# The chunk recurrence of the gated linear attention (B heads): sums of all chunks first, states after them, output parts within chunks meanwhile

## The chip, the cores and the metric

The program runs on one core of a Trainium2 chip. The metric is the device time of one execution in microseconds, from the first to the last instruction of the core; smaller is better. TensorE (PE in the profile) multiplies and turns tiles, VectorE (DVE) and ScalarE (ACT) work on vectors, SyncE (SP) issues the loads of the weights. A core has one SBUF of 128 partitions and a PSUM of 8 banks of 512 float32 per partition, called `ps` here.

## What is computed

The reference is two transformer blocks on 512 tokens of width 1024: two layers with three kinds of heads and a SwiGLU, then two layers with a mixer and a mixture of experts each. The change is in one of the three kinds of heads of the first two layers, the gated linear attention `hgrn2_chunked` (4 heads of 64 by 64). It is shown here as the reference has it, for chunks of 64 tokens; the kernel takes chunks of 128.

```python
def step(state, inp):
    qt, lf, vt = inp
    kt = -jnp.expm1(lf)
    cum = jnp.cumsum(lf, axis=2)
    ...
    attn = jnp.einsum('bhtd,bhsd,bhtsd->bhts', qt, kt, decay)
    o = attn @ vt + jnp.einsum('bhtd,bhde->bhte', qt * jnp.exp(cum), state)
    last = cum[:, :, -1:, :]
    state = jnp.exp(last[:, :, 0, :, None]) * state + jnp.einsum('bhsd,bhse->bhde', kt * jnp.exp(last - cum), vt)
    return state, o
```

The output of a chunk has a part within the chunk (`attn @ vt`) and a part from the state before it. What a chunk adds to the state does not depend on the state. The state before the first chunk is zero.

## The kernel before

Each of the first two layers is a row of stages: `project_in`, `windows` (sliding attention), `hgrn` (the B heads), `delta` (the C heads), `project_out`, `swiglu`. Between stages PE, DVE and ACT meet at a barrier. Each engine has its own copy of each stage as a list of instructions written by hand, and they are tied by counting semaphores: `due("name")` gives the count to wait for, `signal` and `to("name", ...)` raise it, and `link` makes an engine wait for its own instruction. Each engine runs its list in order. The weights come as 1 MB panels through a ring of 8 places; SP issues a panel as soon as PE has released the place (`panel_used`), line 629.

The stage `hgrn` works on tiles with features on the partitions: two blocks `b` of 128 partitions, each with two heads `s` of 64 partitions, and 512 tokens in four chunks `c` of 128. Its first part builds the scores `attn` level by level, with four panels of modulation weights (`mod_panels`) multiplied in between. Its end, which the change touches, runs so:

- DVE line 2411 puts each token's distance to the end of its chunk into `b_d` (signal `b_qd`).
- ACT line 1770 takes `b_e` = exp(`b_cum`), line 1771 takes `b_d` = exp(-`b_d`) and signals `b_decay`, line 1772 takes each chunk's whole decay, lines 1775 and 1776 move score blocks between partitions (`b_spread`), `row_out(3, 7)` (line 1751) copies a modulation vector, and line 1779 copies the turned k out of PSUM banks 4 and 5 (`b_kdT_sb`).
- DVE waits for `b_decay`, then line 2413 multiplies `b_e` by q, line 2414 multiplies `b_d` by k (signal `b_kd`), line 2415 clears the state.
- PE turns `b_d` (`chunk_turns`, eight turns through line 655, signal `b_kdT`), turns the modulation vector (`mod_turn(3, 7)`, two turns), and then for each chunk, having waited for `b_state`: 16 products 64 columns wide into banks 0 and 1 (for each block, head and half of the chunk one of the state with the decayed q, and one of v with the scores, added in place), and, except in the last chunk, two products 128 columns wide of what the chunk adds (bank 4, signal `b_ds`). All go through `mm`, line 641. A float32 product is two records in the trace: 64-column products have the form `128*64 128x64`, the ones of what a chunk adds `128*128 128x128`.
- DVE, for each of the first three chunks, waits for `b_ds`, masks the sum by heads (line 2418), and takes the new state block by block (line 2421, two instructions), signal `b_state`. In the first chunk it also copies the modulation columns (`columns_out`, line 2334) after that.
- After the last chunk PE multiplies the identity by itself once (signal `b_out`), and ACT copies banks 0 and 1 to `mix` (line 1781). After the barrier `delta` begins with twelve small turns.

The loop of PE before, in short:

```python
for c in range(NT):
    pe.wait_ge(*due("b_state"))
    for b in range(2):
        for s in range(2):
            r = slice(s * 64, s * 64 + 64)
            for at, scores in ((c * P, b_left), (c * P + 64, b_near)):
                mm(ps[r, b, at:at + 64], b_s[:, b, r], b_e[:, b, at:at + 64], True, False)
                mm(ps[r, b, at:at + 64], b_vt[:, c, b * P + s * 64:b * P + s * 64 + 64],
                   scores[:, s, b * 4 + c, :], False, True)
```

`r` picks the half of the partitions of PSUM that a product writes, and so the half of the columns of the array that it uses: head `s` = 0 the lower, `s` = 1 the upper.

Of the kernel before, what the change touches and what calls it, by code (L numbers as in the profile page):

```python
# [11 lines left out]
ALU = mybir.AluOpType  # L12
# [6 lines left out]
P = 128  # L19
# [283 lines left out]
def build(nc, args, out, par):  # L303
    a = args
    general, first_t, even_t, pool_t = (packed(t)[1] for t in constants())
    with ExitStack() as ctx:
# [30 lines left out]
        def cut(buffer, start, size, **shape):  # L337

            v = buffer[:, start:start + size]
            if not shape:  # L340
                return v
            names_ = " ".join(shape)
            return v.rearrange(f"p ({names_}) -> p {names_}", **shape)
# [53 lines left out]
        b_vt, b_kdt = cut(work, 3072, 1024, c=4, f=256), cut(work, 4096, 1024, c=4, f=256)  # L397
        b_s, b_tmp = cut(work, 5120, 256, b=2, e=P), cut(work, 5376, 256, b=2, e=P)

# [235 lines left out]
        def _(pe):  # L635
# [276 lines left out]
            def hgrn(l):  # L912
# [31 lines left out]
                pe.wait_ge(*due("b_kdT_sb"))  # L944
                pe.wait_ge(*due("b_acc", 0))
                for c in range(NT):
                    pe.wait_ge(*due("b_state"))
                    for b in range(2):
                        for s in range(2):
                            r = slice(s * 64, s * 64 + 64)  # L950
                            for at, scores in ((c * P, b_left), (c * P + 64, b_near)):
                                mm(ps[r, b, at:at + 64], b_s[:, b, r], b_e[:, b, at:at + 64], True, False)
                                mm(ps[r, b, at:at + 64], b_vt[:, c, b * P + s * 64:b * P + s * 64 + 64],
                                   scores[:, s, b * 4 + c, :], False, True)
                    if c < NT - 1:
                        for b in range(2):
                            mm(ps[:, 4, b * P:b * P + P], b_kdt[:, c, b * P:b * P + P], b_vt[:, c, b * P:b * P + P],
                               True, True, "b_ds" if b else None)
                mm(ps[:, 5, 0:P], ident, ident, True, True, "b_out")

# [593 lines left out]
        def _(act):  # L1554
# [203 lines left out]
            def hgrn():  # L1758
                act.wait_ge(*due("b_v"))
                to("b_v_sb", f(b_vt, ps[:, 4:6, :].rearrange("p b (c f) -> p (b c) f", c=2), ACT.Copy))  # L1760
                for n in range(len(LEVELS)):
# [5 lines left out]
                    if n in (2, 5):  # L1767
                        row_out(1 + n // 3, 7)
                act.wait_ge(*due("b_qd"))
                link(f(b_e, b_cum, ACT.Exp))  # L1770
                to("b_decay", f(b_d, b_d, ACT.Exp, scale=-1.0))
                link(f(stats[:, 32:40].rearrange("p (b c) -> p b c", b=2),
                       b_cum.rearrange("p b (c t) -> p b c t", c=4)[:, :, :, P - 1], ACT.Exp))
# [415 lines left out]
        def _(dve):  # L2189
# [175 lines left out]
            def hgrn(l):  # L2365
# [45 lines left out]
                to("b_qd", tt(blocks_of(b_d, P), c, c[:, :, P - 1:P].to_broadcast([P, 8, P]), ALU.subtract))  # L2411
                dve.wait_ge(*due("b_decay"))
                link(tt(b_e, q, b_e, ALU.mult))
                to("b_kd", tt(b_d, z, b_d, ALU.mult))
                to("b_state", dve.memset(b_s, 0.0))
                for c in range(NT - 1):
                    dve.wait_ge(*due("b_ds"))
                    link(tt(b_tmp, ps[:, 4, 0:256].rearrange("p (b e) -> p b e", b=2),
                            halves.unsqueeze(1).to_broadcast([P, 2, P]), ALU.mult))
                    for b in range(2):  # L2420
                        i = stt(out=b_s[:, b, :], in0=b_s[:, b, :], scalar=stats[:, 32 + 4 * b + c:33 + 4 * b + c],
                                in1=b_tmp[:, b, :], op0=ALU.mult, op1=ALU.add)
                    to("b_state", i)
                    if c == 0:
                        columns_out(PLANS[f"layer{l}"], 3, 7)
                    due("b_state")
                due("b_state")
# [730 lines left out]
```

## Time and profile before

| what | value |
|---|---|
| runs | 3260.21, 3258.86, 3250.52 us |
| median | 3258.86 us |
| profiled execution | 3258.9 us, its span; nothing is shown around it |
| PE busy | 2947.2 us (90%) |
| DVE busy | 1062.4 us (33%) |
| ACT busy | 913.0 us (28%) |
| DMA | mean 196 GB/s, about 409 GB/s in the expert layers |
| granted TensorE clock | 0.962 of full speed in the mean |

How to read it: the busy shares say which engine works most, the chain of waits says which instruction ended last at each step, and the timeline gives start, duration, engine, line and, in square brackets, the idle time before an instruction and who ended it. The granted clock is given as a share of 2.4 GHz: 1.00 is 2.4 GHz and 0.50 is 1.2 GHz; a value between is a stretch with both.

### The profile page before, as it was taken

The numbers are of one execution on the slowest core, as the hardware profiler recorded it, in microseconds if no ns is written. First come the engines' busy times: TensorE is split into PE (matmuls) and PEld (weight loads), VectorE is DVE, ScalarE is ACT, GpSimd is POOL, SyncE is SP. The second block draws the span as 40 slices with busy tenths as digits, with TensorE's granted clock in tenths as the row PEclk, the third lists the DMA queues.
The fourth block names the chain that finished last, engine by engine and source line by source line (L and its number), as shares of the span: only waits on it lengthen the run. The fifth ranks groups of instructions, "written<-read, shape, count | busy, mean of one in ns | idle before, by whom it ended". The sixth has DMA issues, their size and how long they took to land.

```text
span 3258.9 us, 41546 instructions
## 1 busy us (share of the span) xinstructions
PE 2947.2 (90%) x18407; PEld 2024.4 (62%) x18407; DVE 1062.4 (33%) x1573; ACT 913.0 (28%) x1498; POOL 0.2 (0%) x4
## 2 busy tenths in 40 slices
PE   6997899999998799999989998889898887999897
PEld 3765768888776677888767766654443454444443
DVE  3445642233545653224243244420010135000002
ACT  3443242232444333223243354221110032110011
POOL 0000000000000000000000000000000000000000
PEclk9998999999999899999989999989999998999999
DMA  7224323323223422322263105479999953999997
GB/s 273 78 104 156 105 65 95 99 88 97 78 90 113 156 71 78 101 93 91 94 217 124 39 1 207 142 291 410 409 407 408 406 210 117 388 409 409 403 408 291
DMA packets 251539, 637.28 MB, mean 196 GB/s; under 512 B 12896, under 2 KB 110176, under 8 KB 251232
## 3 DMA queue, kind: packets, MB, share of 16 engines
q1 hardware_dynamic: 248224, 627.22, 51.9%
q10 hardware_dynamic: 3136, 7.40, 0.6%
q8 instruction: 146, 2.39, 0.3%
q14 instruction: 33, 0.27, 0.0%
HBM read 632.48 MB, written 2.10 MB: 195 GB/s over the span
## 4 chain that ended last, share of the span: by engine, by line
PE 70%; DMA 12%; DVE 7%; ACT 5%; PEld 2%; issue 2%; PEldq 1%; SPq 1%; ACTq 0%; DVEq 0%
PE ps L641 67%; DMA ring<-in_w_exp_up 6%; DMA ring<-in_w_exp_gate 5%; PE ps L655 3%; PEld ps L641 2%; ACT h L1653 1%; ACT mix_halves L1656 1%; PEldq L1112 1%; DMA ring<-in_ada_w 1%; SPq L629 0%; DVE work L2394 0%; DVE work L3038 0%; DMA ring<-in_w_mod 0%; DVE small L2952 0%; DVE work L2954 0%
## 5 line engine op out<-in xcount | busy, mean ns | idle before, releaser
L641 PE MATMUL ps<-mix_halves,work_halves 128*128 128x512 f32 (+1 forms) x1544 | 622.5, 403 | 44.7 <-DVE h_halves L2245 34.4
L641 PE MATMUL ps<-h_halves,work_halves 128*128 128x512 f32 (+1 forms) x1544 | 609.7, 395 | 6.2 <-DVE mix_halves L2245 3.9
L641 PE MATMUL ps<-mix_halves,ring_halves 128*128 128x512 f32 x1448 | 569.1, 393 | 0.0
L641 PE MATMUL ps<-ring,work 128*64 128x512 f32 x1552 | 395.5, 595 | 57.5 <-DMA ring<-in_w_exp_up 31.6
L2245 DVE TENSOR_TENSOR ring_halves<-ring,work_halves 128x2048 fp32r<-128x2048 f32 (+2 forms) x125 | 252.6, 2021 | 551.9 <-ACT work_halves L1576 453.5
L641 PEld LDWEIGHTS ps<-mix_halves,work_halves 128*128 128x128 f32 (+1 forms) x1544 | 291.1, 189 | 131.9 <-issue 49.2
L641 PEld LDWEIGHTS ps<-h_halves,work_halves 128*128 128x128 f32 (+1 forms) x1544 | 291.9, 189 | 73.8 <-issue 6.4
L641 PEld LDWEIGHTS ps<-mix_halves,ring_halves 128*128 128x128 f32 x1448 | 273.0, 189 | 60.8
L641 PEld LDWEIGHTS ps<-ring,work 128*64 128x64 f32 x1552 | 129.5, 137 | 270.7 <-issue 269.2
L1576 ACT ACTIVATE work_halves<-ring 128x2048 fp32r<-128x2048 f32 x102 | 188.2, 1845 | 336.7 <-PE ps L641 336.1
L641 PE MATMUL ps<-ring,proj 128*64 128x512 f32 (+1 forms) x1136 | 231.2, 546 | 3.1 <-issue 3.0
L2645 DVE SCALAR_TENSOR_TENSOR x<-ps,small,x 128x512 f32<-128x512 f32 x112 | 81.1, 748 | 291.5 <-PE ps L641 291.3
L641 PEld LDWEIGHTS ps<-ring,proj 128*64 128x64 f32 (+1 forms) x1136 | 81.4, 131 | 131.9 <-issue 126.2
L641 PE MATMUL ps<-proj_halves,work_halves 128*128 128x512 f32 x352 | 136.9, 389 | 0.0
L3010 DVE TENSOR_TENSOR work<-proj,ps 128x1024 f32<-128x1024 f32 x16 | 19.5, 1221 | 345.6 <-PE ps L641 345.6
L2080 ACT ACTIVATE work<-ps,small 128x128 f32<-128x128 f32 x128 | 48.2, 457 | 288.0 <-PE ps L641 288.0
L641 PE MATMUL ps<-proj,work 64*64 64x64 f32 (+3 forms) x1008 | 116.6, 325 | 13.3 <-issue 6.5
L641 PE MATMUL ps<-work,proj 64*64 64x64 f32 (+3 forms) x1488 | 113.1, 254 | 15.2 <-ACT proj L2050 3.4
L641 PEld LDWEIGHTS ps<-work,mix 128*128 128x128 f32 x1024 | 119.1, 197 | 11.0 <-issue 8.1
L641 PE MATMUL ps<-h_halves,ring_halves 128*128 128x512 f32 x320 | 125.8, 393 | 0.0
L641 PE MATMUL ps<-work,mix 128*128 128x128 f32 x1024 | 121.7, 281 | 2.6 <-DVE work L2978 2.6
L641 PE MATMUL ps<-ring,mix 128*32 128x256 f32 x1280 | 87.7, 421 | 33.8 <-DVE mix L2217 20.4
(396 smaller groups left out, 3405.7 us busy)
## 6 DMA issues: line engine op xcount, KB each, us to landing
ring<-in_w_exp_down SPq DMA_DIRECT2D x110, 1024.0 KB, 16.3
ring<-in_w_exp_gate SPq DMA_DIRECT2D x106, 1024.0 KB, 11.0
ring<-in_w_exp_up SPq DMA_DIRECT2D x88, 1024.0 KB, 15.2
ring<-in_ada_w SPq DMA_DIRECT2D x48, 1024.0 KB, 7.4
ring<-in_w_mod SPq DMA_DIRECT2D x48, 1024.0 KB, 7.5
ring<-in_w_in SPq DMA_DIRECT2D x22, 1024.0 KB, 5.3
ring<-in_w_gate SPq DMA_DIRECT2D x22, 1024.0 KB, 5.3
ring<-in_w_up SPq DMA_DIRECT2D x22, 1024.0 KB, 5.3
```

Of the source, the lines that this page charges most:

```text
L641: i = pe.matmul(o, lhsT, rhs, start=start, stop=stop, **kw)
L655: t = pe.transpose(o, i, ident[0:n, 0:n])
L1112: pe.drain().then_inc(sem["stage"], 1)
L1576: to("hi", f(rounded(panel_high(splits[0])), slot(n), ACT.Copy))
L1653: to("h", f(h_[:, k, :], h_[:, k, :], ACT.Identity, scale=scale[:, k:k + 1], bias=shift[:, k:k + 1]))
L1656: to("hi", f(rounded(hi[:, k, :]), h_[:, k, :], ACT.Copy))
L2080: i = f(x_sel[:, k, :], ps[:, 6 + half, k % 4 * P:k % 4 * P + P], ACT.Identity, scale=coef[:, 1, k:k + 1], bias=mod[:, l, 3, k:k + 1])
L2245: to("lo", tt(rounded(v), v, rounded(hi), ALU.subtract))
L2645: to(done, stt(out=x[:, m, :], in0=ps[:, bank, :], scalar=gate[:, m:m + 1], in1=x[:, m, :], op0=ALU.mult, op1=ALU.add))
L3010: to("e_act", tt(e_act, e_tmp, ps[:, 2:4, :].rearrange("p b f -> p (b f)"), ALU.mult))
```

## The change

For each layer's `hgrn` stage:

- ACT takes exp(-`b_d`) first, with its own signal, then exp(`b_cum`), also with a signal. DVE multiplies `b_d` by k after the first, signals `b_kd`, and multiplies `b_e` by q after the second.
- PE issues what all three chunks add in one run (six products of 128 columns, banks 4 and 5, one signal at the end), then the output parts within all four chunks (32 products of 64 columns, the two heads in turn), and then, for chunks 1 to 3, waits for the state and issues four products of 128 columns each. The products with the zero state of chunk 0 and the product of the identity are gone; the last product gives `b_out`.
- DVE copies the modulation columns before it waits for `b_ds`; then it masks the first sum right into the state after chunk 0 (signal), masks the other two into `b_tmp`, and takes the two further states with two instructions each. The clearing of the state is gone. Three states and three sums have places of their own.

```diff
--- before.py
+++ after.py
@@ -395,7 +395,7 @@
         b_near, b_far = (cut(work, at, 1024, s=2, g=8, t=64) for at in (1024, 2048))
         b_mask, b_left = cut(proj_all, 0, 7 * 64, n=7, t=64), cut(proj_all, 1024, 1024, s=2, g=8, t=64)
         b_vt, b_kdt = cut(work, 3072, 1024, c=4, f=256), cut(work, 4096, 1024, c=4, f=256)
-        b_s, b_tmp = cut(work, 5120, 256, b=2, e=P), cut(work, 5376, 256, b=2, e=P)
+        b_s, b_tmp = (cut(work, at, 768, c=3, b=2, e=P) for at in (5120, 5888))
 
         g_Ac, g_Ar, g_Tc, g_Yc = (cut(work, 1024 * i, 1024, g=16, t=64) for i in range(4))
         g_Xc, g_Y = cut(proj_all, 2048, 1024, g=16, t=64), four(work, 4096)
@@ -943,20 +943,24 @@
                 pe.wait_ge(*due("b_spread"))
                 pe.wait_ge(*due("b_kdT_sb"))
                 pe.wait_ge(*due("b_acc", 0))
+                for c in range(NT - 1):
+                    for b in range(2):
+                        at = c % 2 * 256 + b * P
+                        mm(ps[:, 4 + c // 2, at:at + P], b_kdt[:, c, b * P:b * P + P], b_vt[:, c, b * P:b * P + P],
+                           True, True, "b_ds" if c == NT - 2 and b else None)
                 for c in range(NT):
+                    for b in range(2):
+                        for at, scores in ((c * P, b_left), (c * P + 64, b_near)):
+                            for s in range(2):
+                                mm(ps[s * 64:s * 64 + 64, b, at:at + 64], b_vt[:, c, b * P + s * 64:b * P + s * 64 + 64],
+                                   scores[:, s, b * 4 + c, :], at == 0, False)
+                for c in range(1, NT):
                     pe.wait_ge(*due("b_state"))
                     for b in range(2):
                         for s in range(2):
                             r = slice(s * 64, s * 64 + 64)
-                            for at, scores in ((c * P, b_left), (c * P + 64, b_near)):
-                                mm(ps[r, b, at:at + 64], b_s[:, b, r], b_e[:, b, at:at + 64], True, False)
-                                mm(ps[r, b, at:at + 64], b_vt[:, c, b * P + s * 64:b * P + s * 64 + 64],
-                                   scores[:, s, b * 4 + c, :], False, True)
-                    if c < NT - 1:
-                        for b in range(2):
-                            mm(ps[:, 4, b * P:b * P + P], b_kdt[:, c, b * P:b * P + P], b_vt[:, c, b * P:b * P + P],
-                               True, True, "b_ds" if b else None)
-                mm(ps[:, 5, 0:P], ident, ident, True, True, "b_out")
+                            mm(ps[r, b, c * P:c * P + P], b_s[:, c - 1, b, r], b_e[:, b, c * P:c * P + P], False, c == NT - 1,
+                               "b_out" if c == NT - 1 and b and s else None)
 
             def delta(l):
 
@@ -1767,8 +1771,8 @@
                     if n in (2, 5):
                         row_out(1 + n // 3, 7)
                 act.wait_ge(*due("b_qd"))
-                link(f(b_e, b_cum, ACT.Exp))
                 to("b_decay", f(b_d, b_d, ACT.Exp, scale=-1.0))
+                to("b_decay", f(b_e, b_cum, ACT.Exp))
                 link(f(stats[:, 32:40].rearrange("p (b c) -> p b c", b=2),
                        b_cum.rearrange("p b (c t) -> p b c t", c=4)[:, :, :, P - 1], ACT.Exp))
                 near, far, left = (v.rearrange("p s g t -> p (s g t)") for v in (b_near, b_far, b_left))
@@ -2410,20 +2414,23 @@
                 c = blocks_of(b_cum, P)
                 to("b_qd", tt(blocks_of(b_d, P), c, c[:, :, P - 1:P].to_broadcast([P, 8, P]), ALU.subtract))
                 dve.wait_ge(*due("b_decay"))
+                to("b_kd", tt(b_d, z, b_d, ALU.mult))
+                dve.wait_ge(*due("b_decay"))
                 link(tt(b_e, q, b_e, ALU.mult))
-                to("b_kd", tt(b_d, z, b_d, ALU.mult))
-                to("b_state", dve.memset(b_s, 0.0))
-                for c in range(NT - 1):
-                    dve.wait_ge(*due("b_ds"))
-                    link(tt(b_tmp, ps[:, 4, 0:256].rearrange("p (b e) -> p b e", b=2),
-                            halves.unsqueeze(1).to_broadcast([P, 2, P]), ALU.mult))
+                columns_out(PLANS[f"layer{l}"], 3, 7)
+                dve.wait_ge(*due("b_ds"))
+                added = ps[:, 4:6, :].rearrange("p k f -> p (k f)")[:, 0:768].rearrange("p (c b e) -> p c b e", c=3, b=2)
+                mask = halves.unsqueeze(1).to_broadcast([P, 2, P])
+                to("b_state", tt(b_s[:, 0, :, :], added[:, 0, :, :], mask, ALU.mult))
+                for c in (1, 2):
+                    i = tt(b_tmp[:, c, :, :], added[:, c, :, :], mask, ALU.mult)
+                link(i)
+                for c in (1, 2):
+                    dve.wait_ge(*due("b_state"))
                     for b in range(2):
-                        i = stt(out=b_s[:, b, :], in0=b_s[:, b, :], scalar=stats[:, 32 + 4 * b + c:33 + 4 * b + c],
-                                in1=b_tmp[:, b, :], op0=ALU.mult, op1=ALU.add)
+                        i = stt(out=b_s[:, c, b, :], in0=b_s[:, c - 1, b, :], scalar=stats[:, 32 + 4 * b + c:33 + 4 * b + c],
+                                in1=b_tmp[:, c, b, :], op0=ALU.mult, op1=ALU.add)
                     to("b_state", i)
-                    if c == 0:
-                        columns_out(PLANS[f"layer{l}"], 3, 7)
-                    due("b_state")
                 due("b_state")
 
             def project_in(l):
```

## Rows read from the trace of the kernel before

**Rows 1.** The page, part 4, chain that ended last: shares of the span by engine.

```profile
PE 70%; DMA 12%; DVE 7%; ACT 5%; PEld 2%; issue 2%; PEldq 1%; SPq 1%; ACTq 0%; DVEq 0%
```

**Rows 2.** The chain of waits, layer 0, stage hgrn's end: start us, us, what.

```profile
285.33 1.06 ACT h L1770
...
287.51 1.24 DVE h L2413
...
288.77 1.24 DVE h L2414
...
290.14 2.37 PE ps L655 x10
...
293.24 3.71 PE ps L641 x36
...
309.61 1.02 ACT mix L1781
```

**Rows 3.** The chain of waits, layer 1, first and last of that end.

```profile
1084.82 3.71 PE ps L641 x36
...
1101.33 1.02 ACT mix L1781
```

**Rows 4.** Timeline, layer 0: what ACT and PE do around the turns.

```profile
289.67 0.36 ACT L1751 ACTIVATE mix<-ps 128x256 f32<-128x256 f32 x1
...
290.14 1.94 PE L655 MATMUL ps<-consts,h 128*128 128x128 f32 x8 [4.46 <-DVE h L2414]
...
291.88 0.63 PE L655 MATMUL ps<-consts,mix 128*128 128x128 f32 x2
292.12 1.02 ACT L1779 ACTIVATE work<-ps 128x1024 f32<-128x1024 f32 x1 [2.09 <-PE ps L655]
```

**Rows 5.** Windows, layer 0: us, busy PE, PEld, DVE, ACT, POOL; PEclk, DMA share, GB/s.

```profile
285.00:290.00 5.00, 0.59 (x2) 0.11 (x1) 2.75 (x3) 4.57 (x6) 0.00 (x0) 0.89 1.03 409
...
293.00:305.00 12.00, 9.42 (x101) 8.63 (x102) 2.15 (x7) 0.14 (x1) 0.00 (x0) 0.50 0.28 89
...
306.00:307.00 1.00, 0.45 (x4) 0.25 (x3) 0.48 (x2) 0.00 (x0) 0.00 (x0) 1.00 0.00 0
...
312.00:317.00 5.00, 4.66 (x17) 3.19 (x16) 3.49 (x12) 4.35 (x13) 0.00 (x0) 0.58 0.00 0
```

**Rows 6.** Timeline of PE: 64-column products, the two heads overlapping, 1.2 and 2.4 GHz.

```profile
294.18 0.48 PE L641 MATMUL ps<-h,work 128*64 128x64 f32 x4
...
294.67 0.48 PE L641 MATMUL ps<-h,work 128*64 128x64 f32 x4
...
308.18 0.34 PE L641 MATMUL ps<-h,work 128*64 128x64 f32 x4
...
308.47 0.33 PE L641 MATMUL ps<-h,work 128*64 128x64 f32 x4
```

**Rows 7.** Timeline of PE, stage delta, layer 0: 128-column products of two heads.

```profile
384.66 0.69 PE L641 MATMUL ps<-proj,work 128*64 128x128 f32 x4
385.08 0.69 PE L641 MATMUL ps<-h,work 128*64 128x128 f32 x4
385.71 1.22 PE L641 MATMUL ps<-work,proj 128*128 128x128 f32 x4
...
404.44 0.40 PE L641 MATMUL ps<-h,work 128*64 128x128 f32 x4
404.65 0.44 PE L641 MATMUL ps<-proj,work 128*64 128x128 f32 x4
```

**Rows 8.** Groups of instructions by form, 293 to 310 us: xcount, busy us, mean ns.

```profile
L641 PE MATMUL ps<-h,work 128*64 128x64 f32 x64 | 8.4, 304 | 4.2 <-DVE work L2421 3.5 <-issue 0.7
...
L2421 DVE SCALAR_TENSOR_TENSOR work<-work,small 128x128 f32<-128x128 f32 x6 | 1.8, 349 | 0.1
L2418 DVE TENSOR_TENSOR work<-ps,consts 128x256 f32<-128x256 f32 x3 | 1.3, 425 | 14.0 <-PE ps L641 14.0
```

**Rows 9.** Who waited for whom, SP's own queue, whole span.

```profile
SPq L629 <- PE ps L641: 2766.8, 388, 116.7
```

## The prediction

> **What bounds the kernel now.** I read the chain that ended last first: seven tenths of the span are PE, and DVE and ACT have a few per cent each [rows 1]. So a change to one short stage can only matter if that stage itself stands on the chain. The chain of waits over the stage shows that it does, without a gap: two exponentials on ACT, two products on DVE, the turns on PE, four rounds of PE and DVE, and the copy to `mix` [rows 2]. From the first product (293.24) to that copy (309.61) it takes 16.37 us in layer 0, and in layer 1 16.51 us (1084.82 to 1101.33) [rows 3]. Between the rounds PE stands while DVE masks the sum and takes the state. PE's granted clock is the second thing to see: it falls within 285 to 290, where PE is nearly idle, is 0.50 (1.2 GHz) all through 293 to 305, and is back at 1.00 (2.4 GHz) only from 306 on; it falls again in the early part of the next stage [rows 5]. So most of these rounds ran at the half clock. Last, DMA: it is busy for 0.28 of the rounds [rows 5], and SP's own waits are all but entirely waits for PE to free a panel [rows 9]. Nothing here waits for a weight, so what PE saves, later loads are issued earlier by; I take a gain in this stage one to one to the end of the kernel, through the expert layers too, whose loads also follow PE's releases.
>
> **The way in.** Before: exponential (285.33, 1.06), second exponential, product 2413 (1.24), product 2414 (1.24), turns at 290.14 [rows 2]. After: one exponential, one product, turns. So the turns start 1.06 + 1.24 + 0.05 of hand-overs = 2.35 us earlier, at 287.79. Eight turns take 1.94, to 289.73 [rows 4]. Not all of that arrives: ACT has its two copies and `row_out` in the same order as before, and `row_out` starts at 289.67 and takes 0.36 [rows 4]. The copy of the turned k follows at 290.05 instead of 292.12 and takes 1.02, so it ends at 291.07, and PE starts about 0.1 later, at 291.2 instead of 293.24. **Gain 2.05 us.** The product of `b_e` and the modulation columns now stand ahead of DVE's wait for the sums. The first ends at about 288.9; the columns wait for the turn of the modulation vector, which needs `row_out` (290.03) and takes 0.63 on PE [rows 4], to about 290.7, and are copied by 290.9. The sums come after 292, so both are hidden; without that cover they would cost 1.24 and 0.2. The cleared state (a memset beside the turns) and its removal cost nothing, for the same reason. No DMA issue is moved.
>
> **PE, what the chunks add.** Six products of 128 columns are 12 records. A record of 128 columns takes 0.22 us at 1.2 GHz: eight turns, each one record, from 290.14 to 291.88 [rows 4]. 12 x 0.22 = 2.6 us at the half clock, 1.3 at the full one.
>
> **PE, parts within chunks.** 32 products of 64 columns, 64 records. Before, two heads' products already overlap: eight records, four of each head, take 0.49 us at 1.2 GHz (294.18 to 294.67) and 0.29 at 2.4 GHz (308.18 to 308.47) [rows 6]. After, the heads alternate at every product, which should overlap at least as well; 64 / 8 x 0.49 = 3.9 us, or 8 x 0.29 = 2.3. The alternating order as such is not in the trace. Its bounds: with no overlap it is twice as long (+3.9 at the half clock); at the best, eight records pass as four of twice the width do, in 0.42 us [rows 7], which is -0.5. I take the rates of rows 6, since they are the same products in another order.
>
> **PE, products with states.** 12 products of 128 columns, 24 records in place of 64 records of 64 columns. In the next stage four such records take 0.42 us at 1.2 GHz (384.66 to 385.08) and 0.21 at 2.4 GHz (404.44 to 404.65) [rows 7]. 24 / 4 x 0.42 = 2.5, or 1.3. A change of width costs something: the step from the 64-wide to the 128-wide form is 0.63 instead of 0.42 [rows 7]. After, there is one such change (sums to parts) where before each of the first three rounds had one and the identity another: 0.2. The end of the last product and the hand-over to ACT add 0.2; the identity's product (about 0.5 at the end of before) is gone, and that lies in the difference of the ends.
>
> **DVE meanwhile.** Mask 0.43, two more masks 0.85, then two states of two instructions at 0.35 each, 1.3 with hand-overs, 2.7 us in all [rows 8]. The sums end at 293.8 at the half clock, so the last state is there at about 296.7, and PE needs it only after the parts within chunks and two chunks of states, later than 297. Hidden. If PE had the full clock from the start, the sums would end at 292.6, the parts at 294.9, and the last state at 295.4 would come a little late, some 0.3 us: that is what is late next.
>
> **The sum.** All at 1.2 GHz: 2.6 + 0.2 + 3.9 + 2.5 + 0.2 = 9.4, from 291.2 to 300.6, instead of 309.61: 9.0 us a layer. All at 2.4 GHz: sums 1.3, then the DVE chain 2.7, then the last chunk 0.5 and hand-overs 0.3, to 296.1: 13.5 us. Which? Before, the clock was back after the third round, a stretch in which PE had two idle gaps behind it and a last round of 3 us at work. After, PE works from 291.2 on without a gap, so I expect the clock back about halfway, near 295.7: sums and half of the parts at the half clock (2.6 + 0.2 + 1.9), the rest at the full one (1.2 + 1.3 + 0.2), 7.4 us, to 298.6. **Gain 11.0 us a layer, 22 us for two.** The profiled execution is 3258.9 us and the median of the runs 3258.86, so one sum serves for both: 3258.9 - 22 = **3237 us**. One of the three runs is 8 us lower than the other two, so the median itself may be off by some microseconds.
>
> The next stage meets another clock too. Before, it had 2.4 GHz at first and then a stretch of 312 to 317 with 0.58 in the mean [rows 5]. The whole of that at one level or the other moves its 5 us by some 2 to 3 us either way, for each layer; I take nothing and give it to the range.
>
> **The rivals.**
>
> *No help from the clock.* PE stays at 1.2 GHz to the end of the stage, as for 12 us before [rows 5]. Then 9 us a layer, 3241 us, and if the next stage then has more of the low clock, 3246. For it: the clock was slow to come back before [rows 5]. Against: the idle gaps that stood in the rounds are gone. 0.15.
>
> *The clock never falls.* The turns start 2.35 us earlier, so PE's idle stretch before them, which brought the clock down [rows 5], is halved. Then DVE's chain sets the end, 13.5 us a layer, 3232 us, and down to 3227 with a faster next stage. Against: PE was almost idle from 285 to the turns in any case. 0.15. The Trainium skill, "TensorE: Matmul & The Clock Gate" (Part 1), says that the half clock is the default and that recent activity releases it, and by that rule a run of work with no gap favours this rival and the forecast over the first; the trace agrees in that the fall comes with idle PE.
>
> *It is lost again.* The stage gets shorter by what the sum says, but another stage's clock, or a transfer that then ends last, takes over half of it: 3249 to 3256. For it: the clock falls easily, [rows 5] show two falls within 30 us. Against: SP waits for PE, not PE for loads, in all of the layers [rows 9]. 0.07.
>
> *Slower: the halves do not overlap when they alternate.* If each change of the half made PE wait for the whole product before, a 64-column record would cost its full 0.30 us [rows 8] instead of 0.06, and a 128-column one 0.67 at most (the length of a row of four) [rows 7]. 64 x 0.30 + 24 x 0.67 + 2.6 = 38 us against the 18.4 (16.37 + 2.05) that are there: 19 us a layer slower, 3298 us. It decides above a mean of (18.4 - 2.6) / 88 = 0.18 us a record. Against: eight records in 0.49 us, each 0.30 long, can't be had without overlap [rows 6]. 0.03. The Trainium skill, "TensorEngine Tiling (Array Packing)" (Key Properties), has the array drain when the tiling mode changes, not when only the tile does; by it this rival does not happen, and the 0.2 us at the change of width is what it calls a drain.
>
> *The change does not do what it says*, PE waiting for a state before it may start the parts within chunks: the order of the lists excludes it.
>
> **How the numbers follow.** Forecast 0.60, no help 0.15, never falls 0.15, lost again 0.07, slower 0.03. What a measurement of this kernel can tell from no change is about 0.3%, 10 us, so below 3249 counts as faster. All of the first three are (0.90); "lost again" counts as the same (0.07); 0.03 slower. The range takes in the low and the high clock with the next stage on either side, 3227 to 3246; "lost again" and "slower" are outside.
>
> **What would show it.** Turns near 287.8 and the first product 128 wide near 291.2; 12, 64 and 24 records with no idle of PE between; eight records of the parts in 0.3 to 0.5 us; the last state of DVE ahead of its use; the copy to `mix` at 296 to 301 in layer 0, and some 11 us earlier still (22 in all, 1079) in layer 1; the granted clock at 1.00 by 296. Wrong would be: parts within chunks at over 0.12 us a record, PE idle before the products with states by more than 0.5 us, or later stages that give back more than 5 us.

## The result, and the profile after

The changed kernel takes 3226.17 us (median of four runs, 3225.54 to 3227.00). The kernel before, with one more run beside it, takes 3256.39 us. The ratio is 0.9908 with a 95% interval of 0.9894 to 0.9921: **faster by 0.9%, 30 us**. The forecast was 3237 us, 22 us faster, with a range that ended at 3227. The sign was right, and so was what happens in the stage; the size was not: the measured gain lies outside the range, by 0.8 us at its end and by 10.8 us from the forecast.

The chain of waits of the changed kernel, end of stage `hgrn` of layer 1 (start us, us, what), has three rounds less than [rows 2, 3]:

```profile
1066.11 1.06 ACT h L1774
1067.17 0.95 ACT h L1775
1068.11 0.11 ACT small L1776
...
1068.25 1.07 ACT proj L1779
...
1069.34 1.06 ACT work L1780
1070.40 0.28 ACT mix L1755
...
1070.72 0.69 PE ps L655 x2
1071.40 0.27 issue
1071.67 6.71 PE ps L641 x100
...
1078.41 1.02 ACT mix L1785
```

One piece of PE, 100 records without a wait of any other engine, stands where four were. DVE no longer appears. The way in is no longer the two exponentials, two products and the turns: after the first exponential it is ACT's own row (the second exponential, the decays, the copies, down to `row_out`, L1755), and then the turn of the modulation vector on PE.

The timeline of the changed kernel, layer 0, answers to [rows 4, 6]:

```profile
286.95 1.06 ACT L1774 ACTIVATE h<-h 128x1024 f32<-128x1024 f32 x1 [6.21 <-DVE h L2415]
...
289.41 1.06 PE L655 MATMUL ps<-consts,h 128*128 128x128 f32 x8 [2.15 <-DVE h L2417]
...
291.56 0.69 PE L655 MATMUL ps<-consts,mix 128*128 128x128 f32 x2 [1.08 <-ACT mix L1755]
...
292.51 2.90 PE L641 MATMUL ps<-work 128*128 128x128 f32 x12 [0.26 <-issue]
...
295.44 0.42 DVE L2424 TENSOR_TENSOR work<-ps,consts 128x256 f32<-128x256 f32 x1 [2.92 <-PE ps L641]
...
295.61 0.43 PE L641 MATMUL ps<-work 128*64 128x64 f32 x4
...
295.82 0.43 PE L641 MATMUL ps<-proj,work 128*64 128x64 f32 x4
...
296.57 1.26 DVE L2431 SCALAR_TENSOR_TENSOR work<-work,small 128x128 f32<-128x128 f32 x4
...
297.66 0.28 PE L641 MATMUL ps<-proj,work 128*64 128x64 f32 x4
...
297.78 0.28 PE L641 MATMUL ps<-work 128*64 128x64 f32 x4
...
298.13 1.48 PE L641 MATMUL ps<-h,work 128*64 128x128 f32 x24
299.66 1.02 ACT L1785 ACTIVATE mix<-ps 128x1024 f32<-128x1024 f32 x1 [7.25 <-PE ps L641]
```

The 12 records of the sums start at 292.51, the parts follow at 295.34, the products with states at 298.13, the copy to `mix` at 299.66. DVE has the last state at 297.83 (296.57 + 1.26), ahead of the first product with a state.

Windows of the changed kernel (us, busy PE, PEld, DVE, ACT, POOL; PEclk, DMA share, GB/s) answer to [rows 5]:

```profile
290.00:292.00 2.00, 0.92 (x7) 0.52 (x5) 0.40 (x1) 1.97 (x4) 0.00 (x0) 0.62 1.04 424
292.00:297.00 5.00, 4.74 (x46) 4.30 (x45) 1.69 (x6) 0.41 (x1) 0.00 (x0) 0.50 0.61 193
297.00:300.00 3.00, 2.61 (x62) 2.37 (x60) 0.80 (x3) 0.34 (x1) 0.00 (x0) 0.95 0.23 94
300.00:310.00 10.00, 6.84 (x50) 5.57 (x50) 7.04 (x17) 8.19 (x21) 0.00 (x0) 1.00 0.01 2
```

The clock falls to 1.2 GHz within 290 to 292 and is back soon after 297, where before it stayed down for 12 us and more. In the next stage it is now at 2.4 GHz all through 300 to 310.

**Where the time went.** I cut the span at the starts of the same ACT instructions in each profile: the first exponential of the end of `hgrn` and the copy to `mix` at its end, the copy to `mix` at the end of `delta`, the same three in layer 1, and the first squares of x ahead of the expert layers. "Attention" is a part of the stretch before it: from ACT's first copy of turned weights in the even layer's attention (1852.86 before, 1822.55 after) to the third one (1863.53, 1828.63). All in us:

| profile | to the first exponential | end of hgrn 0 | delta 0 | to layer 1's | end of hgrn 1 | delta 1 | to the expert layers | of it attention | rest | span |
|---|---|---|---|---|---|---|---|---|---|---|
| before | 285.3 | 24.3 | 96.4 | 670.8 | 24.4 | 96.4 | 881.1 | 10.7 | 1180.1 | 3258.9 |
| changed | 287.0 | 12.7 | 94.4 | 672.1 | 12.3 | 93.7 | 871.5 | 6.1 | 1181.6 | 3225.2 |

The two profiles differ by 33.7 us. 11.6 + 12.1 = 23.7 of them are in the stage that was changed, 2.1 + 2.7 = 4.8 in the `delta` stages, whose code is the same, and 9.6 in a stretch that begins a stage later. 4.3 are lost in the first, the fourth and the last column, also in unchanged code. So the stage gave what was forecast, 22, and a little more, and some 10 us came from outside it. The medians differ by 30.2 us, 3.5 less than these two profiles, so the parts outside the stage are a few microseconds smaller in the median than here. What they are is the question of the experiments.

### The profile page after: what moved, and what is told of

The parts are those of the page before. It is cut to its first block, busy times and chain, and to the rows that moved or that the text cites. A ratio compares the mean times of both kernels' runs of the same rounds, so it can differ in the third digit from the quotient of the medians.

```text
span 3225.2 us, 41374 instructions
## 1 busy us (share of the span) xinstructions
PE 2927.1 (91%) x18323; PEld 2008.5 (62%) x18323; DVE 1059.7 (33%) x1567; ACT 912.0 (28%) x1498; POOL 0.2 (0%) x4
## 4 chain that ended last, share of the span: by engine, by line
PE 70%; DMA 12%; DVE 6%; ACT 5%; PEld 3%; issue 2%; PEldq 1%; SPq 1%; ACTq 0%; DVEq 0%
PE ps L641 68%; DMA ring<-in_w_exp_up 6%; DMA ring<-in_w_exp_gate 5%; PE ps L655 3%; PEld ps L641 3%; ACT h L1657 1%; ACT mix_halves L1660 1%; PEldq L1116 1%; DMA ring<-in_ada_w 1%; SPq L629 0%; DVE work L2398 0%; DVE work L3045 0%; DVE small L2959 0%; DVE work L2961 0%; DVE h L2386 0%
## 5 line engine op out<-in xcount | busy, mean ns | idle before, releaser
L641 PE MATMUL ps<-work,proj 64*64 64x64 f32 (+3 forms) x1488 | 113.1, 251 | 15.1 <-ACT proj L2054 3.4
L641 PE MATMUL ps<-ring,mix 128*32 128x256 f32 x1280 | 89.9, 432 | 33.1 <-DVE mix L2221 20.4
L641 PE MATMUL ps<-proj,work 64*64 64x64 f32 (+3 forms) x1008 | 107.3, 318 | 13.2 <-issue 6.5
```

The lines of the kernel that those rows point to most:

```text
L641: i = pe.matmul(o, lhsT, rhs, start=start, stop=stop, **kw)
```

## The experiments

**The kernel before, with the way in alone.**

```diff
-                link(f(b_e, b_cum, ACT.Exp))
                 to("b_decay", f(b_d, b_d, ACT.Exp, scale=-1.0))
+                to("b_decay", f(b_e, b_cum, ACT.Exp))
...
-                link(tt(b_e, q, b_e, ALU.mult))
                 to("b_kd", tt(b_d, z, b_d, ALU.mult))
+                dve.wait_ge(*due("b_decay"))
+                link(tt(b_e, q, b_e, ALU.mult))
```

> The kernel before with only the two exponentials and the two products of the way in swapped; the recurrence is the old one. My step: the first product of PE starts 2.05 us earlier after the exponential, in each layer, so the stage (from the first exponential to the copy to mix) takes 22.2 us instead of 24.3, and the kernel 4 us less, about 3252. Rival 'the gain outside the stage is bound to the way in' (the shorter idle stretch of PE keeps the clock up): then the granted clock in the stage is 1.00 for longer, and the kernel gains 8 us or more.

Measured 3251.54 us against 3257.32 for the kernel before beside it, ratio 0.9984 (0.9975 to 0.9994). The stage took 20.4 and 19.1 us, not 22.2. Each way in saved 2.3 us (from the first exponential to the first product 5.57 and 5.56 us, instead of 7.91 and 7.93). The windows of layer 0 say where the rest came from:

```profile
294.00:297.00 3.00, 1.83 (x12) 1.54 (x13) 1.11 (x4) 0.00 (x0) 0.00 (x0) 0.50 0.76 298
297.00:300.00 3.00, 2.86 (x33) 2.55 (x31) 0.10 (x1) 0.00 (x0) 0.00 (x0) 0.59 0.00 0
300.00:303.00 3.00, 1.97 (x36) 1.91 (x36) 0.94 (x3) 0.00 (x0) 0.00 (x0) 1.00 0.02 5
303.00:306.00 3.00, 1.83 (x35) 1.58 (x35) 1.04 (x3) 0.00 (x0) 0.00 (x0) 1.00 0.00 0
```

Two of the four rounds ran at 2.4 GHz here, and three in layer 1, where before it was the last alone. Neither expectation held whole: the clock is part of the gain, but the total of 8 us was not reached.

**The changed kernel, with the recurrence alone** (the way in as before; the diff above, reversed).

> The changed kernel with the old order of the two exponentials and products, so the recurrence alone is new. By my sum the stage takes 12.7 + 2.05 = 14.8 us in layer 0 and the kernel 4 us more than the changed one, 3230. If the earlier turns also set when the granted clock falls and comes back, the difference is larger: the clock is back later, the stage takes up to 17 us, and the kernel 3235.

Measured 3238.72 us, ratio 0.9947 (0.9930 to 0.9964). The stage took 15.1 and 15.4 us, 2.4 to 3.1 more than with the new way in. That is near the 14.8 of the sum, but the kernel is slower than both expectations, 3230 and 3235: it lost 12.5 us against the changed one, not 4. `delta` took 98.8 and 97.4 us instead of 94.4 and 93.7. In the profiles, 5.5 us of what was lost are in the stage and 8.1 in `delta`, whose code neither edit touches. The recurrence alone gives 18.6 us of 30 (3257.32 - 3238.72); the way in alone 5.8. They don't add up, and what is missing lies outside: in the stage itself the profiles give 18.2 and 9.2 us, more together than the 23.7 of both parts in one kernel.

**Products with states in two halves.**

```diff
-                            mm(ps[r, b, c * P:c * P + P], b_s[:, c - 1, b, r], b_e[:, b, c * P:c * P + P], False, c == NT - 1,
-                               "b_out" if c == NT - 1 and b and s else None)
+                            for at in (c * P, c * P + 64):
+                                mm(ps[r, b, at:at + 64], b_s[:, c - 1, b, r], b_e[:, b, at:at + 64], False, c == NT - 1 and at > c * P,
+                                   "b_out" if c == NT - 1 and b and s and at > c * P else None)
```

> The changed kernel with each product with a state cut into two of 64 columns: 48 records for 24, the same columns. If products are paid by columns and the change of width is what costs (theory), 6 groups of eight at 0.29 us are 1.75 instead of 1.48 us: 0.3 us a layer, no difference in the kernel's time. If each record has its own price of 0.06 us whatever its width (rival), 48 x 0.06 = 2.9 us, 1.4 us a layer, 3 us in all.

Its timeline of PE, layer 0:

```profile
296.80 0.28 PE L641 MATMUL ps<-work 128*64 128x64 f32 x4
296.92 1.62 PE L641 MATMUL ps<-h,work 128*64 128x64 f32 x48
```

48 records take 1.62 us where 24 of twice the width took 1.48. So the time goes with the columns and not with the number of records, and "128 wide" is worth 0.14 us a layer. The kernel took 3228.60 us (ratio 0.9918, 0.9901 to 0.9936), no difference that can be told. This profile had the long form of the attention stretch, 10.7 us, and 98.7 us of `delta` in layer 0.

**The heads two by two instead of in turn.**

```diff
-                        for at, scores in ((c * P, b_left), (c * P + 64, b_near)):
-                            for s in range(2):
+                        for s in range(2):
+                            for at, scores in ((c * P, b_left), (c * P + 64, b_near)):
```

> The changed kernel with the parts within chunks in the old order of heads: two products of one head, then two of the other, instead of head by head in turn. Forecast took the same rate for both orders (0.49 us for eight records at 1.2 GHz); the profile of the changed kernel shows 0.43. If the alternating order is what made that, this run shows 0.49 at 1.2 GHz again and the parts take 0.3 to 0.4 us longer a layer; if the order does not matter, the parts keep 0.43. The kernel's time changes by under 1 us either way.

Timeline of PE, layer 0:

```profile
294.47 0.48 PE L641 MATMUL ps<-proj,work 128*64 128x64 f32 x4
294.68 0.48 PE L641 MATMUL ps<-work 128*64 128x64 f32 x4
294.89 0.48 PE L641 MATMUL ps<-proj,work 128*64 128x64 f32 x4
```

Four records start every 0.21 us, eight every 0.43, the same as with the heads in turn. So the order of the heads does not matter, and it is not what made 0.43 of the 0.49 of [rows 6]. What did is open. Before, two products in a row wrote the same 64 columns of a bank; after, none do in any of the runs with the new recurrence. No run isolates that. The kernel took 3223.28 us (ratio 0.9901, 0.9880 to 0.9923), as the changed one.

**Useless work in the stage.** The changed kernel with 14 products of the identity ahead of the end, and with 56:

```diff
-                               "b_out" if c == NT - 1 and b and s else None)
+                               None)
+                for _ in range(14):
+                    mm(ps[:, 6, 0:P], ident, ident, True, True, "b_out" if _ == 13 else None)
```

> The changed kernel with 14 products of the identity (128 columns, into an unused bank) ahead of the last signal of the stage, in both layers: 14 x 0.213 = 3.0 us of dense work at 2.4 GHz, 6 us in all, that nothing else needs. Theory (the surplus of the change lies in stages that it does not touch and comes from where the granted clock happens to fall in them): the stage gets 3 us longer in each layer, and the rest of the kernel moves by several us either way, so the total is not 3226 + 6 but anything from 3226 to 3242. Rival (the surplus is a steady gain of the change): the rest keeps its time within 2 us, 3232.

> The same with 56 products, 12.0 us a layer, about what the change saves there: the stages after it stand nearly where they stood before the change. Theory: the total may come near the kernel before, 3250 to 3258, with the delta stages starting at 2.4 GHz. Rival (steady surplus outside the stage): 3226 + 24 = 3250 with the stretch from the second delta stage to the second half of the even layer as short as in the changed kernel, 872 us.

With 14 products: 3239.54 us (3236.84 to 3240.74; ratio 0.9939, 0.9920 to 0.9957). 6 us were added, 13 came. With 56: 3260.07 us, ratio 1.0008 (0.9996 to 1.0019). 24 us were added, 34 came; the execution that was profiled is the fastest of its ten, and its span is 27.7 us above the changed kernel's. The stage itself got 3.3 and 3.5 us longer with the one, 12.6 and 12.3 with the other, as it should. The rest stopped being fast: the stretch to the expert layers went from 871.5 to 876.3 and 875.8, its attention part from 6.1 to 10.7 in both. That speaks against a steady gain outside the stage. The `delta` stages do not tell the same story: 95.0 and 93.8 us with 56 products, nearly as short as in the changed kernel. What is in common to the two runs is the attention's fall.

**The same two kernels, profiled again.**

> The changed kernel as it is, profiled once more. Theory: the end of the hgrn stage is again 12.3 to 12.9 us long, and the other stretches differ from the first profile by up to 5 us each where the granted clock falls elsewhere. Rival: all stretches agree within 1 us, so that what differs from the kernel before is the change's own.

> The kernel before as it is, profiled once more. Theory: the end of the hgrn stage takes 23.5 to 24.5 us again, while the stretch from the second delta stage to the second half of the even layer, 881 us in the first profile, comes out anywhere from 871 to 882. Rival: it is 881 again, and a stage there is slow in the kernel before for a reason of its own.

Measured 3224.55 and 3256.90 us. The stretches of all profiles, cut as above:

| profile | end of hgrn 0 | delta 0 | end of hgrn 1 | delta 1 | to the expert layers | of it attention | span |
|---|---|---|---|---|---|---|---|
| before | 24.3 | 96.4 | 24.4 | 96.4 | 881.1 | 10.7 | 3258.9 |
| before, again | 23.0 | 96.2 | 25.9 | 97.1 | 876.5 | 10.7 | 3255.6 |
| changed | 12.7 | 94.4 | 12.3 | 93.7 | 871.5 | 6.1 | 3225.2 |
| changed, again | 12.2 | 93.8 | 12.3 | 93.7 | 868.7 | 6.1 | 3222.3 |
| way in alone | 20.4 | 96.7 | 19.1 | 96.3 | 874.8 | 10.6 | 3244.7 |
| recurrence alone | 15.1 | 98.8 | 15.4 | 97.4 | 874.6 | 10.5 | 3241.1 |
| states 64 wide | 12.8 | 98.7 | 12.7 | 95.3 | 877.5 | 10.7 | 3232.9 |
| heads two by two | 12.7 | 94.4 | 12.3 | 93.5 | 872.1 | 6.1 | 3220.7 |
| 14 useless products | 16.1 | 95.9 | 15.7 | 96.8 | 876.3 | 10.7 | 3237.2 |
| 56 useless products | 25.3 | 95.0 | 24.6 | 93.8 | 875.8 | 10.7 | 3252.9 |

Neither expectation is quite it. The long stretch varies from profile to profile of one kernel, by 4.6 us before and 2.8 after. So does the end of `hgrn` in the kernel before: 24.3 and 24.4 us the first time, 23.0 and 25.9 the second, both outside the 23.5 to 24.5 that were expected. In layer 1 of the second profile the granted clock stays at 0.50 through all four rounds:

```profile
1082.00:1100.00 18.00, 14.29 (x142) 12.84 (x142) 3.19 (x10) 0.11 (x1) 0.00 (x0) 0.50 0.18 60
```

So where the clock comes back can differ between two executions of one kernel. The attention part is another matter: it has two lengths and nothing between, and a kernel had the same one both times; `delta` was the same within 0.7 us. These two lengths repeated with the kernel, although their code is the same in both. The two kernels with 6.1 us in this table are the two whose earlier stages have nearly the same lengths; a third one further down, with stages of 10.5 us and nothing changed in the attention, has 6.1 us too. I have two profiles each of only two kernels, which is little for "always".

**The attention stretch.** PE's rows in the kernel before and in the changed one:

```profile
1844.75 1.57 PE L641 MATMUL ps<-h,proj 64*128 64x512 f32 x8 [1.20 <-ACT h L1985]
1848.61 2.74 PE L641 MATMUL ps<-h,proj 64*128 64x512 f32 x4 [2.29 <-ACT work L1991]
```

```profile
1816.29 1.57 PE L641 MATMUL ps<-h,proj 64*128 64x512 f32 x8 [1.19 <-ACT h L1989]
1820.15 1.55 PE L641 MATMUL ps<-h,proj 64*128 64x512 f32 x4 [2.29 <-ACT work L1995]
```

The same products after the same 2.29 us of idle PE take 2.74 us in the one and 1.55 in the other. The "attention" column begins behind them, so it misses the first part of the fall: from the start of the eight products to the third copy it is 18.78 us in the kernel before (both profiles) and 12.34 in the changed one. **The whole fall costs 6.4 us there**, not the 4.6 of the column. In the five other kernels with 10.5 to 10.7 in the column it is 17.1, 4.8 us more than in the changed one: there the products behind the idle stretch still take 1.55 us, and the fall comes behind them. The granted clock, by the windows of the kernel before and then of the changed one:

```profile
1848.00:1853.00 5.00, 4.39 (x11) 2.38 (x12) 0.69 (x3) 1.69 (x5) 0.00 (x0) 0.58 0.43 170
1853.00:1862.00 9.00, 9.00 (x34) 5.29 (x36) 2.08 (x4) 3.59 (x8) 0.00 (x0) 0.50 0.00 0
```

```profile
1820.00:1825.00 5.00, 4.85 (x21) 2.84 (x22) 1.40 (x4) 3.11 (x9) 0.00 (x0) 1.00 0.36 147
```

To test that it is the idle stretch and the clock, and nothing that the change brings, I filled the stretch with two useless products, in the kernel before:

```diff
                 scores(0)
                 scores(1)
+                for _ in range(2):
+                    mm(ps[:, 6, 0:512], ident, proj[:, 6, :], True, True)
                 for i in range(tiles):
```

> The kernel before with two dummy products of 512 columns (1.7 us at 2.4 GHz) in PE's idle stretch of 2.3 us at the start of the even layer's attention. Theory (there the same products ran at 1.2 GHz in the kernel before and at 2.4 GHz in the changed one, only because of where the clock fell): the stretch that took 10.7 us before and 6.1 in the changed kernel takes 6.1 here, and the kernel gains 4 to 5 us, 3252. Rival: it stays 10.7, and something that the change brings about makes it short.

```profile
1841.63 1.99 PE L641 MATMUL ps<-proj,consts 128*128 128x512 f32 x4
1843.99 1.55 PE L641 MATMUL ps<-h,proj 64*128 64x512 f32 x4 [0.37 <-ACT work L1993]
```

The products behind the filler take 1.55 us, and the stretch 6.1 us instead of 10.7; from the eight products to the third copy it is 12.34 us, as in the changed kernel. The kernel before as a whole takes 3252.89 us against 3258.53 beside it (ratio 0.9988, 0.9976 to 1.0000), which agrees, but just reaches no change at all. So the 6.4 us of the surplus that lie in this stretch are not a merit of the change: two lines elsewhere in the old kernel make the stretch as short.

The same filler in the kernel with 14 useless products:

> The changed kernel with 3.0 us of dense filler in each hgrn stage, as measured at 3239.5, and the attention filler. Theory: its attention stretch goes from 10.7 to 6.1 us and the kernel to 3235. Rival: it stays at 3239.

The attention stretch is again 6.1 us, and the kernel 3232.76 us (3229.84 to 3239.49; ratio 0.9917, 0.9895 to 0.9940), an interval that overlaps the one without the filler (0.9920 to 0.9957). Its profile, at 3237.7, shows none of that gain in the whole, since from the third copy to the expert layers it is 3.4 us longer, and from there to the end 2.3. So the stretch is settled and the sum of all is not.

**Keeping the clock in the stage itself.** The changed kernel with useless products in the two idle stretches of the way in:

```diff
                 pe.wait_ge(*due("b_acc", 2))
+                for _ in range(2):
+                    mm(ps[:, 6, 0:512], ident, proj[:, 6, :], True, True)
                 pe.wait_ge(*due("b_kd"))
                 chunk_turns(b_d, 2, 4, "b_kdT")
+                for _ in range(2):
+                    mm(ps[:, 6, 0:256], ident, proj[:, 6, 0:256], True, True)
                 mod_turn(3, 7)
```

> The changed kernel with dummy products of PE in two idle stretches of the way in: two of 512 columns (1.7 us at 2.4 GHz) before the turns, two of 256 (0.85 us) between the turns of k and that of the modulation vector. Nothing reads them. Theory (the way in lets the clock fall, and the sums and half of the parts then run at 1.2 GHz): the granted clock stays at 1.00, the sums take 1.4 us instead of 2.8, DVE's chain of masks and states sets the end, and the stage takes 10.3 to 11.0 us instead of 12.3 to 12.7, 3 to 4 us for two layers. Rival (the fall does not come from the idle stretch): no shorter, or longer by the filler.

```profile
294.77 1.58 PE L641 MATMUL ps<-work 128*128 128x128 f32 x12 [0.52 <-issue]
...
298.19 1.48 PE L641 MATMUL ps<-h,work 128*64 128x128 f32 x24
299.72 1.02 ACT L1789 ACTIVATE mix<-ps 128x1024 f32<-128x1024 f32 x1 [5.05 <-PE ps L641]
```

The sums take 1.5 us instead of 2.8, and the stage 10.51 us in both layers, 2.2 and 1.8 less than in the changed kernel. The granted clock is 1.00 all through, and the attention stretch is 6.1 us. Even here DVE's states come in time: its last instructions (297.50 to 298.77) end before the last eight of the 24 records, which use that state and begin at about 299.1. So PE sets the end, and not DVE's chain, as was expected. The kernel takes 3220.88 us, ratio 0.9889 (0.9867 to 0.9911). With the attention filler as well:

> The changed kernel with both fillers. Theory: 3 to 4 us less in the two hgrn stages, the attention stretch 6.1 us as in the changed kernel; the delta stages and others may land elsewhere, so 3220 give or take 6, against 3226 for the changed kernel. Rival (clock elsewhere sets it): no better than 3226.

3217.72 us, ratio 0.9874 (0.9852 to 0.9895), the fastest of all and **41 us below the kernel before beside it**. The changed kernel has 0.9908 (0.9894 to 0.9921) by itself. The intervals just touch, so I claim no more than the 4 us that the stage's rows show.

## Why the prediction was right or wrong

- **What bounds the stage.** Right: PE and DVE in turn, all of it on the chain. After, PE alone, with no gap.
- **What bounds the rest.** "SP waits for PE, not PE for loads, in all of the layers" is a wrong reading: [rows 1] have DMA with 12% of the chain, and in the expert layers of the kernel before PE waits 56.7 us for the weights of the experts (37.5 and 19.2). The conclusion drawn from it did hold there: from the start of the expert layers to the end it is 1180.1 us before and 1181.6 after, so what comes earlier into them comes out earlier.
- **The way in.** Forecast 2.05 us. From the first exponential to the first product it was 7.91 us before (285.33 to 293.24) and is 5.56 after (286.95 to 292.51): 2.35. The limit that the text named, ACT's `row_out`, was the right one. The turns themselves ran at 2.4 GHz, 1.06 us instead of 1.94, which the forecast had not used, and which gained little, since `row_out` came later than both.
- **The sums.** 2.6 and 0.2 for the change of width; measured 2.8 (292.51 to 295.34). Right.
- **The parts within chunks.** Half at each clock, 1.9 + 1.2 = 3.1; measured 2.8 (295.34 to 298.13). The rate was 0.43 instead of 0.49 us for eight records at 1.2 GHz, the lower bound given was 0.42. The order of the heads, which the text named as what the trace does not show, does not matter.
- **The products with states.** 1.5 with the hand-over; measured 1.53. Right.
- **The clock in the stage.** Forecast back at 4.5 us into the dense run; it was at about 4.7 (292.5 to 297.2). In the 16 stage ends of this kind that ran into the low clock (eight profiles with the new recurrence), it was 3.1 to 5.5 us after the first product; in six of the eight with the old one (four profiles) it was 3.7 to 13 us, and in two not before the end. So the clock can come back as soon with the rounds too, but with the dense run it was never late. That this is the term that decides among 9, 11 and 13.5 us a layer held as well: the filler run, with no fall, gave 10.51 us, 13.8 less than the 24.3 of before. DVE's chain, which the text had some 0.3 us late in that case, was in time. "Never falls" was a right price for a case that did not happen.
- **Sum of the stage.** 22.0 us forecast, 23.7 measured in the profiles (23.7 and 24.4 for the two pairs of them).
- **The step that failed** is the last of the sum: "I take nothing and give it to the range" for the next stage, and "one to one to the end of the kernel" for all others. `delta` gave 4.8 us, and the stretch to the expert layers 9.6, of which 6.4 are one fall of the clock in the attention. The other columns took 4.3 back. For the next stage the text had 2 to 3 us a layer either way; the clock of all later ones it named only as something that loses time ("lost again"). It should have had 10 us on both sides. The trace of the kernel before had rows for that, far from the change:

```profile
1600.00:1650.00 50.00, 40.59 (x249) 28.34 (x247) 12.61 (x21) 14.95 (x28) 0.00 (x0) 0.90 0.37 124
1650.00:1700.00 50.00, 41.15 (x220) 32.43 (x221) 25.00 (x50) 25.09 (x42) 0.00 (x0) 0.86 0.70 249
...
1850.00:1900.00 50.00, 50.00 (x318) 31.50 (x316) 17.59 (x35) 26.09 (x56) 0.00 (x0) 0.88 0.01 3
```

The last of them holds most of the attention's fall, which is not there in the changed kernel. That the first two are places of this kind as well is not shown.

- **The two filler runs show the size of that term.** 6 and 24 us of work cost 13 and 34. So these two changes by a known amount came out 7 and 10 us off it. Others were nearer: the filled `hgrn` stage, 4 us shorter in its rows, gave 5.3 us in the medians.
- **The slower rival** (halves that do not overlap in turn) is refuted: 0.054 us a record at 1.2 GHz against the 0.18 at which it decides. The rule of the Trainium skill, "TensorEngine Tiling (Array Packing)" (Key Properties), that changing only the tile needs no drain, fits that row; the change from products that use 128 columns of the array to those that use 64 cost 0.2 us (2.83 us from the first of the sums to the first of the parts, less 2.6 for 12 records), as rows of before had it.
- **The base.** The span of the profiled execution and the median are not the same thing (in every later run the time is 1.7 to 1.8 us above the span of that execution, 3227.0 and 3225.2 for the changed kernel). One sum for both held to 2.5 us all the same: the kernel before had 3256.39 with the fourth run, and 3256.60 to 3258.53 in three later sets. Its runs spread over 3249 to 3266, those of the changed kernel over 3223 to 3230.

Shown by runs: both parts of the change gain, the width of the products hardly matters, the order of the heads does not, filling the idle stretch keeps the clock up in this stage and in the attention, and a part of the measured surplus goes when the stage's length changes. Not settled: why `delta` was 2 to 3 us shorter in the changed kernel. The shortness is gone with 14 useless products ahead of it (95.9 and 96.8) and nearly back with 56. The granted clock is the likely cause: over the 28 `delta` stages of the 14 profiles, those with a mean of 0.94 to 0.96 take 92.2 to 94.4 us (one of them 96.2), those with 0.91 to 0.93 take 95.0 to 97.1, and those with 0.89 and 0.90 take 97.4 to 98.8. But no run filled its idle stretches. Nor is it known why the attention's clock falls in some kernels and not in others, when PE does the same just before.

## What to carry to other kernels

Take out of a recurrence all that does not depend on the state, run it in one piece, and put the state's chain beside it on another engine: here each chunk's round trip of PE and DVE went, and the clock was back within 3.1 to 5.5 us of the first product, where with the rounds it took up to 13 us or did not come back in the stage. Before counting a gain of some ten microseconds, cut both profiles at the same instructions, and see how much of it lies in the stage that was changed; what lies elsewhere may go with the next edit. And where PE idles ahead of a dense piece, as for 2.29 us in this attention, useless products into a spare bank are a cheap test of what the clock costs there.

## What the runs showed that I had not expected

- The same code can have or not have a fall of the clock, and in the attention that repeated with the kernel: the stretch was 6.1 us, or 10.5 to 10.7, and never between, in 14 profiles; in 11 of them its code is the same, and in the other three, with the filler, it was always 6.1. The Trainium skill, "TensorE: Matmul & The Clock Gate" (Part 1), explains variation of this kind by a monitor that runs free of the program; that would fit a length that changes from run to run of one kernel. The two repeats of the attention do not show that, but the end of `hgrn` in the kernel before does (24.3 and 24.4 us, then 23.0 and 25.9).
- Useless work of 3 us a layer cost the kernel twice as much as it lasts, while the stage itself got longer only by about what it lasts (3.3 and 3.5 us).
- Eight 64-column records of two heads take 0.43 us at 1.2 GHz, and 0.23 to 0.24 at 2.4 GHz, where the old sequence took 0.49 and 0.29.
